# Attention probabilities scaled on TensorE, by diagonal matrices of reciprocals, instead of by a GpSimd product

## The reference

```
scores = q . k * HEAD_DIM ** -0.5 + relative-position bias      (-1e30 outside the window)
m      = max(max(scores, axis=-1), sink)
p      = exp(scores - m)
denom  = sum(p, axis=-1) + exp(sink - m)
probs  = p / denom
out    = probs . v
```

## Time and profile before

| | |
|---|---|
| median of 3 runs | 2708.9 us (2707.06 to 2710.8) |
| profiled execution, span | 2706.0 us (its own time beside the span is not given) |
| TensorE busy | 2569.1 us, 95% |
| VectorE busy | 1288.9 us, 48% |
| ScalarE busy | 877.0 us, 32% |
| GpSimd busy | 282.7 us, 10% |
| chain that ended last | PE 79%, DVE 12%, issue 4%, ACT 3%, DMA 2%, POOL 1% |
| attention stage | 1504.84 to 1713.68 us of the span |

### The profile page before, as it was taken

One profiled execution on the slowest core, in us unless ns is written; L12 is line 12 of the kernel. 1 busy time (PEld: TensorE's weight loads), 2 busy tenths in 40 slices (PEclk: granted clock), 3 DMA queues, 4 the chain that ended last, 5 costly groups with the idle time before them and its releaser, 6 DMA issues.

```text
span 2706.0 us, 39679 instructions
## 1 busy us (share of the span) xinstructions
PE 2569.1 (95%) x15074; PEld 2452.0 (91%) x15074; DVE 1288.9 (48%) x1803; ACT 877.0 (32%) x1559; POOL 282.7 (10%) x386
## 2 busy tenths in 40 slices
PE   5999888999999999999899799899999999999998
PEld 4999887999999999999789455698999999999998
DVE  7566546432342333343766889436333333333432
ACT  3554523421331331222443455324313312311211
POOL 2011233000000000002320133221000000000000
PEclk7999889999999999999999889999999999999999
DMA  3111110111111111111251300011111111111112
GB/s 108 40 40 39 39 39 25 54 37 49 47 39 47 47 41 45 47 43 43 46 78 32 118 1 1 16 39 39 43 43 48 43 41 54 39 41 53 39 43 81
DMA packets 220401, 121.96 MB, mean 45 GB/s; under 512 B 22429, under 2 KB 217949, under 8 KB 220220
## 3 DMA queue, kind: packets, MB, share of 16 engines
q1 hardware_dynamic: 218068, 117.19, 14.8%
q10 hardware_dynamic: 2196, 3.74, 1.2%
q0 software_dynamic: 64, 0.05, 0.0%
HBM read 112.31 MB, written 10.55 MB: 45 GB/s over the span
## 4 chain that ended last, share of the span: by engine, by line
PE 79%; DVE 12%; issue 4%; ACT 3%; DMA 2%; POOL 1%; SPq 0%; ACTq 0%; DVEq 0%; POOLq 0%
PE ps L640 25%; PE ps L642 25%; PE ps L641 25%; DVE stat L1761 1%; DMA raw<-in_w_q 1%; PE ps L910 1%; DVE stat L1748 1%; DVE rstd L1409 1%; DVE nlo L1440 1%; DVE convin L1432 1%; DVE y L1432 1%; DVE pb L1739 1%; PE ps L952 1%; DVE wlo L1404 1%; PE ps L813 0%
## 5 line engine op out<-in xcount | busy, mean ns | idle before, releaser
L640 PE MATMUL ps<-nhi,whi 128*128 128x384 f32 (+1 forms) x3312 | 1096.0, 331 | 65.9 <-POOL nlo L1858 26.8
L642 PE MATMUL ps<-nhi,wlo 128*128 128x384 f32 (+1 forms) x3312 | 1086.2, 328 | 0.0
L641 PE MATMUL ps<-nlo,whi 128*128 128x384 f32 (+1 forms) x3312 | 1085.7, 328 | 0.0
L640 PEld LDWEIGHTS ps<-nhi,whi 128*128 128x128 f32 x3312 | 626.5, 189 | 85.2 <-issue 70.7
L641 PEld LDWEIGHTS ps<-nlo,whi 128*128 128x128 f32 x3312 | 627.0, 189 | 1.6 <-issue 0.2
L642 PEld LDWEIGHTS ps<-nhi,wlo 128*128 128x128 f32 x3312 | 626.4, 189 | 0.0
L1404 DVE TENSOR_TENSOR wlo<-raw,whi 128x1024 fp32r<-128x1024 f32 (+2 forms) x220 | 244.9, 1114 | 623.4 <-ACT whi L1019 623.3
L642 PE MATMUL ps<-hhi,wlo 128*128 128x384 f32 (+1 forms) x1152 | 375.9, 326 | 0.0
L640 PE MATMUL ps<-hhi,whi 128*128 128x384 f32 (+1 forms) x1152 | 375.8, 326 | 0.0
L641 PE MATMUL ps<-hlo,whi 128*128 128x384 f32 (+1 forms) x1152 | 375.6, 326 | 0.0
L1019 ACT ACTIVATE whi<-raw 128x1024 fp32r<-128x1024 f32 (+2 forms) x220 | 208.3, 947 | 448.9 <-PE ps L642 439.7
(11 more groups left out here) (242 smaller groups left out, 2188.3 us busy)
## 6 DMA issues: line engine op xcount, KB each, us to landing
raw<-in_f_w_up SPq DMA_DIRECT2D x96, 512.0 KB, 3.8
raw<-in_f_w_down SPq DMA_DIRECT2D x64, 384.0 KB, 3.5
raw<-in_a_w_in SPq DMA_DIRECT2D x16, 512.0 KB, 4.0
xrows<-in_x_prompt SPq DMA_DIRECT2D x8, 512.0 KB, 6.5
raw<-in_a_w_out SPq DMA_DIRECT2D x8, 512.0 KB, 4.1
raw<-in_w_q SPq DMA_DIRECT2D x16, 256.0 KB, 3.7
raw<-in_w_o SPq DMA_DIRECT2D x32, 128.0 KB, 2.9
strip<-strip_sb ACTq DMA_DIRECT2D x1, 3072.0 KB, 33.9
```

The costliest lines, as they stand in the source:

```text
L640: pe.matmul(out, whi[s][:, w], mhi[:, k, chunk(c)], start=(k == 0), stop=False)
L641: pe.matmul(out, whi[s][:, w], mlo[:, k, chunk(c)], start=False, stop=False)
L642: last = pe.matmul(out, wlo[s][:, w], mhi[:, k, chunk(c)], start=False, stop=(k == nk - 1))
```

## The change

The in-place product on GpSimd goes. VectorE, right after the reciprocals of step i, waits for them and writes for each head (or half of the decode step) a 128x128 diagonal matrix of reciprocals: the identity times the reciprocals, both broadcast, 4 x 128 elements per partition (2 x 128 in the decode step), in one of two halves of `t2`. It then signals `p_ready`. TensorE multiplies each block of the unscaled exponentials by that matrix, as an ordinary fp32 product, where it had multiplied it by the identity in transpose mode. `inv_ready` is gone.

```
+        def scaled_eye(i):
+            return t2[:, ds((i % 2) * 512, 512)].rearrange("p (j q) -> p j q", j=4)
...
 TensorE, transposes(i)
+                eye = scaled_eye(i)
...
-                            last = pe.transpose(ps[:, 4 + h, j * P:(j + 1) * P], pb[i % NPB][:, j, h * P:(h + 1) * P],
-                                                ident[:, :])
+                            last = pe.matmul(ps[:, 4 + h, j * P:(j + 1) * P], pb[i % NPB][:, j, h * P:(h + 1) * P],
+                                             eye[:, j, :], start=True, stop=True)
...
-                        pe.transpose(ps[:, 4, h * P:(h + 1) * P], flat[:, h * LS:h * LS + WIN], ident[:, :])
-                        last = pe.transpose(ps[0:DEC_T, 5, h * P:(h + 1) * P], flat[:, h * LS + WIN:(h + 1) * LS],
-                                            ident[:, :])
+                        pe.matmul(ps[:, 4, h * P:(h + 1) * P], flat[:, h * LS:h * LS + WIN], eye[:, h, :],
+                                  start=True, stop=True)
+                        last = pe.matmul(ps[0:DEC_T, 5, h * P:(h + 1) * P], flat[:, h * LS + WIN:(h + 1) * LS],
+                                         eye[:, h, :], start=True, stop=True)
...
 VectorE, after_exp(i)
-                dve.reciprocal(st[:, 6, 0:m], st[:, 5, 0:m]).then_inc(inv_ready, 1)
+                seq.mark(dve.reciprocal(st[:, 6, 0:m], st[:, 5, 0:m]))
+                seq.settle()
+                eye = ident[:, :].rearrange("p (o q) -> p o q", o=1).broadcast_to([P, m, P])
+                inv = st[:, 6, 0:m].rearrange("p (j o) -> p j o", o=1).broadcast_to([P, m, P])
+                dve.tensor_tensor(scaled_eye(i)[:, 0:m, :], eye, inv, ALU.mult).then_inc(p_ready, 1)
...
 GpSimd
-                pool.wait_ge(inv_ready, i + 1)
-                pool.tensor_tensor(w, w, inv.broadcast_to([P, m, w.shape[2]]), ALU.mult).then_inc(p_ready, 1)
```

More of the change, by code:

```diff
@@ L248, in build @@
         exp_done = sem("exp_done")
-        inv_ready = sem("inv_ready")
         p_ready = sem("p_ready")
```

## The result

| | before | after |
|---|---|---|
| median | 2708.0 us of 4 runs (2707.0 to 2710.8) | 2729.8 us of 4 runs (2728.1 to 2731.3) |
| profiled execution | span 2706.0 | 2731.3 us, span 2729.5 |
| stage, from the first scores to the first product behind it | 1504.84 to 1716.35: 211.5 us | 1509.01 to 1739.94: 230.9 us |

The ratio is 1.0071, with a 95% interval of 1.0053 to 1.0090: the change makes the kernel 21.8 us slower. Of the 23.5 us between the two spans, 19.4 lie in the attention stage. Behind the stage the two traces agree within 0.1 us. Ahead of it, in code that is the same in both, the second is 4.2 us later; over the twelve traces of this case, whose code ahead of the stage is the same, the stage starts anywhere from 1502.9 to 1509.4 us, so I take this part for scatter.

The account below looks back on a forecast made before the run. VectorE's 5.54 us step, stalled beside GpSimd, outlasted TensorE's 4.80; after the change TensorE would bound. Added records 27.6 + half clock 0.8 - idle 13.7 - stretches 2.9 = +11.8 on 2708.9: 2720.7, stated 2720.5 us; 8-in-10 range 2705 to 2728.

Parts of the forecast that it names:

- TensorE becomes the bound: Attention stage: TensorE's full step becomes 5.68 us against VectorE's 4.54, so TensorE bounds all but the first steps.
- VectorE's side: VectorE's full attention step: 1.71 us of stall goes, a 0.69 us product delays later work 0.71 us; 5.54 becomes 4.54.
- Idle time won back: Attention stage: of TensorE's 18.8 us of idle time 5.1 are left, so 13.7 us are won.
- Added records: TensorE's products with the diagonal in attention: 256 added records at 0.108 us each, 27.6 us more.
- Clock: TensorE's half-clock times in attention: first few added records cost 0.8 us more, two stretches that go win 2.9 us.
- two stretches at half clock go: Half-clock stretches at 1550.79 and 1700.52 us, following TensorE's idle time, go: 1.35 + 1.58 = 2.9 us won.
- the sum: Net change of the attention stage: 27.6 + 0.8 - 13.7 - 2.9 = +11.8 us.
- likeliest case's own range: Whole kernel's time if the forecast itself holds, given 70 in 100: 2714 to 2727 us.
- A: Rival: TensorE keeps 2.4 GHz through the stretches after decode steps, saving 13.2 us: 2707.5 us; 13 in 100.
- B: Rival: a TensorE product costs one record, or its second hides behind weight loads: -16.6 us, 2692 us; 8 in 100.
- C: Rival: VectorE bounds again, its broadcast product slow (over 1.83 us); at 2.5 us, 2741 us; 6 in 100.
- D: Rival: a TensorE product takes as long as four transposes: 55 us more, 2776 us; 3 in 100.

Follow-up runs that it names:

- third run: Kernel after, with VectorE writing each set of diagonal matrices twice, a wait between: 2732.7 us, ratio 1.0083.
- first run: Kernel after, with TensorE transposing by the identity again; diagonal matrices written but unused, so no division by the sums: 2702.1 us, ratio 0.997.
- seventh run: Kernel after, with exponentials and diagonal matrices stored and multiplied as fp32r, one record per product: 2709.6 us, ratio 0.9993.
- second run: Kernel before, with ordinary fp32 products by the identity in place of the transposes: 2732.9 us, ratio 1.0082.
- 5: Kernel after, with a decode step's values products laid between the scores products issued ahead of them: 2738.6 us, ratio 1.0092.
- 8: Kernel after, with a decode step's two products of 128 weight columns ahead of the two with 8: 2731.6 us (one run).
- 10: Kernel after, with a decode step's values products streaming 128 columns instead of 32: 2742.7 us, ratio 1.0115.
- run 4: Kernel before, with VectorE's tail of step i-1 (sum and reciprocal) moved behind the negation of step i: 2706.0 us, ratio 0.9981.
- 6: Kernel before, with the negation ahead of VectorE's tail and a decode step's values products interleaved with scores: 2711.1 us, ratio 0.9989.
- 9: Kernel before, with the negation ahead of VectorE's tail and a decode step's values products streaming 128 columns: 2712.1 us, ratio 1.0003.

## Why the prediction was right and where it was too small

The direction, the bound and the mechanism were right. Point by point:

- **TensorE becomes the bound**: right. The idle time of the middle groups is 0.6 us each, VectorE waits 1.20 us in a full step for TensorE, and doubling VectorE's product changes the time by no more than the intervals allow (third run).
- **VectorE's side**: right within 0.02 us: product 0.69 (0.69 forecast), later start of L1753 0.73 (0.71), negation 0.16, step 4.56 (4.54). It is worth 7 us by itself (2709.4 to 2702.1, first run) when TensorE's half is not there.
- **Idle time won back**: 13.7 forecast, 22.0 - 8.5 = 13.5 measured over a stage that here reaches to the next product, with the same wait of 3.14 us at its end in both kernels.
- **Added records**: the count of 256 is right, the price too small. The prediction put it at 0.108 us, with 0.117 as its upper end, from scores with 64 rows. In a full step it is 0.96 / 8 = 0.12, and in a decode step 0.22. The first blocks' products run at half clock, where four added records cost 2.01 - 1.04 = 0.97 us, so 0.48 at full clock. At full clock that is 28 x 0.96 + 4 x 0.48 + 4 x 0.89 = 32.4 us instead of 27.6: 4.8 us more.
- **Clock**: "two stretches at half clock go", 2.9 us won, was wrong as a sum. Those two did go, but the one behind the second decode step grew from 6.8 to 10.1 us, and a new one lies across the last decode step's values:

```profile
1733.93 0.42 PE L964 MATMUL ps<-pt,cv 128*64 128x32 f32 x2
1734.28 0.42 PE L966 MATMUL ps<-pt,vnew 8*64 8x32 f32 x2
```

There a pair takes 0.35 us instead of 0.23 (1734.28 - 1733.93). Over the stage 211.51 x 0.13 = 27.5 us were lost to the clock before and 230.93 x 0.12 = 27.7 after (each good to 1 us, as the clock is given to two places): nothing won, where 2.9 - 0.8 = 2.1 had been set down. That is 2.3 us more.

So the steps of the sum that were off are the record price (4.8 us), the clock (2.3) and the idle time (0.2): together 7.3 us, and they turn +11.8 us into the +19.4 us of the stage within the rounding. TensorE's busy time says the same: it rose by 222.42 - 189.55 = 32.9 us where the sum had 27.6 + 0.8 - 2.9 = 25.5. Up to the end of the last copy, as the prediction measured the stage, it is 1737.27 - 1509.01 = 228.3 us long, not 220. The other 2 us of the measured 21.8 lie within the scatter ahead of the stage and of the medians. The measured median, 2729.8, lies 1.8 us above the upper end of the range that I gave (2728), and 2.8 us above the likeliest case's own range.

Of the rivals, A (the clock holds) did not happen: the clock fell in every one of the kernels tried. (Its price is 13.3 us by its own terms, not 13.2.) B (one record) would have needed another number format, and even then, in the seventh run, the clock took back its 16.6 us: 2709.6, not 2692, with TensorE busy 205.84 us of the stage instead of 189.55 for as many records. C is shown wrong by the product's 0.69 us and by the third run. D, four transposes' time for a product, would be 1.02 + 24 x 0.108 = 3.6 us a step where the rows show 1.98: the rule of the Trainium skill from which it came ("TensorE: Matmul & The Clock Gate", section "Terms") does not hold for blocks of 128 columns here; the factor is 1.98 / 1.02 = 1.9.

The two halves of the change, put together from the runs: VectorE and GpSimd first -7 us (2709.4 to 2702.1), then TensorE +28 us (to 2729.8); in the other order TensorE +24 us (2709.4 to 2732.9, second run), then VectorE and GpSimd -3 us. The first half is worth less once TensorE is the bound.

## What to carry to other kernels

When work moves onto the engine with the least idle time, count its records there before anything else: 256 records at 0.12 us are more than the whole 22 us of idle time that a better feed could win. A stall that comes from two engines' instructions lying side by side (1.87 us for four numbers per partition beside the GpSimd product) can be moved away by order alone, which added nothing to TensorE's queue and gave the only complete version faster than both kernels. And a gain of TensorE's time need not be a gain of the same size while its clock falls in the same loop: 12.6 us of idle time won came out as 3.4 us.

## What the runs showed of the hardware

- TensorE's clock falls to 1.2 GHz at each of the first three decode steps in all twelve traces, and stays there for 6.6 to 20.4 us while the engine is busy without a break. In the kernels with two-record fp32 products (after and runs 2, 3, 5, 8, 10) the stretches last 10.0 to 16.9 us; in those with transposes (before and runs 1, 4, 6, 9) 6.6 to 20.3; with fp32r products of one record 20.4, three times. The ranges overlap, and run 4 alone has 6.6, 16.9 and 20.3 us in one trace, so what sets the length is not shown.
- The fall came in a decode step's values products or less than 1 us behind them in every kernel, with 32 columns or 128, in one run or interleaved with scores. Stretches also began elsewhere: before at 1549.9 and 1700.2 us, around waits of TensorE of 1.39 and 2.10 us, each 3.5 us long.
- Alternating weights of 128 and of 8 columns made four products take 1.47 us, the same four sorted by width 1.18 us.
- An fp32 record of 128 columns costs 0.12 us in a run of products with 128x128 weights, and 0.18 us in the alternating values products with 64 columns of weights.
